# Grid attention: transposing the probabilities in two halves of 64 rows, into two banks, in the tile mode of the scores

## The chip, the core and the metric

The kernel is one program on 1 core of one Trainium2 chip. The metric is the time of an execution on the device in microseconds (us). In the profile, PE is TensorE (PEld its weight loads), DVE is VectorE, ACT is ScalarE, POOL is GpSimd, SP is SyncE.

## The reference

The reference is two transformer blocks, one after the other, on 1024 tokens of width 1024 in float32. The first block has an even layer (window attention with a sink, and differential attention) and an odd layer (latent attention and neighbourhood attention); the second has a dilated attention beside a state-space branch. The change is in the odd layer's neighbourhood attention, called grid in the kernel. Tokens are a grid of 16 rows and 64 columns; eight heads of width 64 attend to 8 x 16 neighbours and to 256 context tokens:

```python
def row_fn(args):
    r, qr = args
    rs = jnp.clip(r - kr_n // 2, 0, rows - kr_n)
    ks = lax.dynamic_slice_in_dim(kg, rs, kr_n, axis=1).reshape(B, n_loc, H, d)
    vs = lax.dynamic_slice_in_dim(vg, rs, kr_n, axis=1).reshape(B, n_loc, H, d)
    ...
    s_loc = jnp.einsum('bqhd,bkhd->bhqk', qr, ks).astype(jnp.float32) * scale + bias[None]
    s_loc = jnp.where(mask, s_loc, NEG)
    s_ctx = jnp.einsum('bqhd,bchd->bhqc', qr, kc).astype(jnp.float32) * scale
    p = jax.nn.softmax(jnp.concatenate([s_loc, s_ctx], axis=-1), axis=-1).astype(v.dtype)
    return (jnp.einsum('bhqk,bkhd->bqhd', p[..., :n_loc], vs)
            + jnp.einsum('bhqc,bchd->bqhd', p[..., n_loc:], vc))
```

## The kernel before

The grid stage works through 32 pairs: four pairs of heads (`hp`), and for each eight blocks of 128 queries (`t`), 8 grid columns of all 16 rows. A pair has two lanes, one head each. Its keys are the neighbouring blocks of 128 and two blocks of context: three and two in the middle (t = 1 to 6), two and two at the edges (t = 0 and 7). One block of keys of one lane is a tile of probabilities, 128 queries x 128 keys, so a pair has ten tiles, or eight at an edge: 24 x 10 + 8 x 8 = 304 tiles.

For each pair:

- `scores` (L1863, PE): for each lane and piece of keys (384 or 256 local ones, then 256 of the context) a product of 64 contracted rows. Lane 0 stands in array rows 0 to 63 and lane 1 in 64 to 127. Each piece has a bank of PSUM, four banks a pair. A product in float32 is two records in the trace (two passes); a transpose is one.
- `minima` (L2963, DVE): adds the bias or mask, scales, writes the row into SBUF (`pair_slot`, in RP) and keeps a running minimum; four a pair, local pieces first, the lanes in turn. It frees the bank.
- `exponential` (L3444, ACT): one for each lane, in place, with the sum in an accumulator column.
- `turn_chunk` (L1876, PE): transposes the tiles, four to a chunk and a bank. The tile is the loaded operand, the identity the one that is streamed.
- `turned_chunks` (L3456 on ACT, L2977 on DVE): copies a chunk from PSUM to one of four slots of 512 columns in RP (`pair_turned`).
- `pair_values` (L1891, PE): products of the values (64 loaded columns) with a turned tile, lane 0 into output partitions 0 to 63 of bank 7, lane 1 into 64 to 127, accumulated over the blocks of keys.
- `pair_outputs` (L3467, ACT): copies the result, 128 x 128, into the block of outputs.

The order of each engine is written by hand. In the step of pair u, PE issues the scores of pair u+1, the values of pair u-1 and the transposes of pair u. DVE does the minima of u+1 and then its copies of u. ACT does the first exponential of u+1, the outputs of u-1, its copies of u and the second exponential of u+1. An engine's queue is strictly in order.

PSUM banks are given out by rings (class `Ring`): `main` has the banks 0 to 4, `turn` the banks 5 and 6. A fill is numbered when the plan is made and waits until the fill that had its bank before was read. `plan_pairs` numbers the fills of `main` in the order: scores of u+1, then what `turns` of u take of it. A pair of ten tiles has three chunks: four tiles in `turn` (read by ACT), four in `turn` (read by DVE), two in `main` (read by ACT). A pair of eight has the first two alone:

```python
cuts = list(range(len(tiles) % 4 if kind == "diff" else 0, len(tiles), 4))
...
if kind in HALVES and c >= 2:
    ch["ring"] = main
elif kind in HALVES:
    ch["f"] = turn.new("dve" if c else "act")
```

A copy also waits until the values have used the chunk that had its slot four chunks before (`s_chunk`). POOL builds the bias tables for a pair of heads (L1270 to L1281) two pairs of heads ahead and stores each finished block of outputs (L1324).

Of the kernel before, what the change touches and what calls it, by code (L numbers as in the profile page):

```python
# [15 lines left out]
ACT = mybir.ActivationFunctionType  # L16
# [3 lines left out]
P = 128  # L20
# [8 lines left out]
HD = 64  # L29
# [85 lines left out]
def build(nc, io, out):  # L115
    x, ctx_in = io["x"][0], io["ctx"][0]
    ctx = ExitStack()
    with ctx:
# [28 lines left out]
        RP = sb("RP", 7168)  # L147
        RX = sb("RX", 3 * 1024)
        RS = sb("RS", 4 * 512)
        ident = sb("ident", P)  # L150
# [21 lines left out]
        ACROSS = ('grid',)  # L172
# [384 lines left out]
        def plan_pairs(kind, pairs, scale, asides=()):  # L557

            todo = list(asides)
            for at, u in enumerate(pairs):  # L560
                u["at"], u["g"] = at, pair_count[0]
                pair_count[0] += 1
                if u["first"]:
                    block_count[0] += 1
                u["block"] = block_count[0] - 1
                u["w"] = sum(pc["w"] for pc in u["pieces"])
                u["aside"], u["turns"] = None, []
                if kind not in ACROSS:
                    divided[0] += 1
                    u["divided"] = divided[0]  # L570
                u["rq"] = new_rms() if kind == "diff" and at == len(pairs) - 1 else None
                tiles = [(lane, P * j, kt) for j, kt in enumerate(u["key_tiles"]) for lane in range(2)]
                if kind == "latent":
                    tiles.sort()
                if kind == "diff":
                    tiles = [x for x in tiles if x[0] == 0]
                cuts = list(range(len(tiles) % 4 if kind == "diff" else 0, len(tiles), 4))
                cuts = ([0] if cuts[0] else []) + cuts + [len(tiles)] if cuts else [0, len(tiles)]
                n = len(cuts) - 1
                for c in range(n):  # L580
                    ch = {"ring": turn, "c": chunk_count[0], "tiles": tiles[cuts[c]:cuts[c + 1]]}
                    if kind in HALVES and c >= 2:
                        ch["ring"] = main
                    elif kind in HALVES:
                        ch["f"] = turn.new("dve" if c else "act")
                    else:
                        ch["f"] = turn.new("act" if c % 2 or (n == 3 and c == 2) or kind == "diff" else "dve")
                    u["turns"].append(ch)
                    chunk_count[0] += 1
                u["turned"] = [[ch for ch in u["turns"] if any(x[0] == lane for x in ch["tiles"])][-1:] for lane in range(2)]  # L590
# [34 lines left out]
            for at, u in enumerate(pairs):  # L625
                if at + 1 < len(pairs):
                    nxt = pairs[at + 1]
                    number_scores(nxt)
                    ask(nxt, at, 4 if kind in HALVES else 6)
                if kind in HALVES:  # L630
                    for c, ch in enumerate(u["turns"][2:]):
                        ch["f"] = main.new("dve" if c else "act")
                    if at >= 2 and kind not in ACROSS:
                        pairs[at - 2]["back"] = main.new("dve")
# [416 lines left out]
        def pair_turned(c):  # L1051

            return RP[:, 5120 + c % 4 * 512:5632 + c % 4 * 512]

        def pair_out(g):

# [392 lines left out]
        def _(pe):  # L1449
# [201 lines left out]
            for si, st in enumerate(stages):  # L1651
# [197 lines left out]
                elif k in PAIRS:  # L1849
# [18 lines left out]
                    def turn_chunk(u, ch):  # L1868
                        if k == "diff":
                            pe.wait_ge(s_mix, u["at"] + 1)  # L1870
                        else:
                            pe.wait_ge(s_pexp, 2 * u["g"] + 1 + max(x[0] for x in ch["tiles"]))
                        ring = ch["ring"]
                        ring.wait_free(pe, ch["f"])
                        for i, (lane, at, _) in enumerate(ch["tiles"]):
                            last = pe.transpose(ring.bank(ch["f"])[:, i * P:(i + 1) * P],  # L1876
# [3 lines left out]
                    def pair_values(u, chunks):  # L1880
# [1 line left out]
                        pe.wait_ge(s_ot, u["g"])  # L1882
                        n_last = len(u["key_tiles"]) - 1
                        for ch in u["turns"][chunks]:
                            ch["ring"].wait_drained(pe, ch["f"])
                            for i, (lane, at, kt) in enumerate(ch["tiles"]):
                                p_t = pair_turned(ch["c"])[:, i * P:(i + 1) * P]
                                vc = u["vc"][lane]
                                first, final = at == 0, at == n_last * P
                                if k in HALVES:  # L1890
# [2 lines left out]
                                else:  # L1893
                                    last = pe.matmul(bank_o[:, P * lane:P * lane + P], p_t, u["v"][:, kt, vc:vc + P],  # L1894
                                                     start=first, stop=final)
                            last.then_inc(s_chunk, 1)

                    def turn_back(u):
                        pe.wait_ge(s_ot, u["g"] + 1)
# [354 lines left out]
        def _(dve):  # L2254
# [429 lines left out]
            for si, st in enumerate(stages):  # L2684
# [241 lines left out]
                elif k in PAIRS:  # L2926
# [40 lines left out]
                    def turned_chunks(u, chunks):  # L2967

                        for ch in chunks:
                            ring = ch["ring"]  # L2970
                            if ring.side[ch["f"]] != "dve":
                                continue
                            ring.wait_full(dve, ch["f"])
# [25 lines left out]
                    def pair_y(u):  # L2999
# [11 lines left out]
                            dve.wait_ge(s_ystore[u["block"] % 2], 16 * (u["block"] // 2))  # L3011
                        dve.wait_ge(s_rec, u["divided"])
                        if k == "latent":
                            dve.wait_ge(s_chunk, u["turns"][-1]["c"] + 1)
                            o = pair_block(st, u["block"])[:, u["y"]:u["y"] + 2 * P].rearrange("p (l c) -> p l c", l=2)
                            r = recips[:, u["at"] % 3, :].unsqueeze(2).broadcast_to([P, 2, P])
                            sig(tt(o, bank_o[:, 0:2 * P].rearrange("p (l c) -> p l c", l=2), r, ALU.mult), s_ot, att_latent["pairs"][0]["g"])
# [122 lines left out]
        def _(act):  # L3140
# [132 lines left out]
            for si, st in enumerate(stages):  # L3273
# [153 lines left out]
                elif k in PAIRS:  # L3427
# [18 lines left out]
                    def turned_chunks(u, chunks):  # L3446

                        for ch in chunks:
                            ring = ch["ring"]
                            if ring.side[ch["f"]] != "act":  # L3450
                                continue
                            ring.wait_full(act, ch["f"])
# [5 lines left out]
                    def pair_outputs(u):  # L3458

                        if k == "latent":  # L3460
                            return
                        act.wait_ge(s_chunk, u["turns"][-1]["c"] + 1)
                        if k == "diff" or k in ACROSS:
                            if u["first"] and u["block"] >= 2:
                                act.wait_ge(s_ystore[u["block"] % 2], 16 * (u["block"] // 2))
# [135 lines left out]
```

## Time and profile before

| | us |
|---|---|
| median of 3 runs | 2604.52 (2602.23 to 2605.28) |
| the profiled execution's own time | 2602.48 |
| its span, first to last instruction | 2600.5 |
| mean granted clock of TensorE, share of full speed | 0.996 |
| PE, DVE, ACT, POOL busy | 2543.1, 1515.0, 799.3, 242.3 |
| grid stage, 1499.40 to 1616.60 of the span | 117.20 |

A matmul's end in the trace is modelled, so starts are what is safe to count: in the timeline the distance from the start of one group of records to the start of the next is what the first one costs PE. Groups of PE are given as engine, line, operands, tile mode (array rows * columns), moved shape and count. The chain of waits goes back from the last instruction to what released it; a bracket `[0.17 <-issue]` is idle time before a group that nothing shown in the profile ended.

### The profile page before, as it was taken

The page shows a single profiled execution, that of the slowest core. Times are in us where ns is not written, and L with a number is a line of the kernel's source. Part 1 is how long each engine was busy: PE and PEld are TensorE (multiplying, and loading weights), DVE is VectorE, ACT ScalarE, POOL GpSimd, SP SyncE. Part 2 cuts the span into 40 slices and gives each one's busy share as a digit, 9 for nine tenths or more (in the row PEclk, how much of TensorE's full clock was granted, in tenths as well). Part 3 has the DMA queues.
Part 4 walks back from the last instruction along what each step waited for, and adds up shares of the span by engine and source line. Part 5 has one row for each costly group of instructions (what it writes and reads, how often), then busy time and mean ns, then how long its engine had stood idle before and what let it go on. Part 6 is the DMA issues. An engine that isn't in the chain of part 4 may idle for free.

```text
span 2600.5 us, 37230 instructions
## 1 busy us (share of the span) xinstructions
PE 2543.1 (98%) x13959; PEld 1865.6 (72%) x13959; DVE 1515.0 (58%) x3827; ACT 799.3 (31%) x1753; POOL 242.3 (9%) x426
## 2 busy tenths in 40 slices
PE   6999999999999999999999999999999999999999
PEld 3477688777778686566688777868578776545867
DVE  2357677599866664344453466757868574515554
ACT  2236511177721123322210066113312364121211
POOL 0100100000001000000042022320000002012000
PEclk9999999999999999999999999999999999999999
DMA  7031000021013121311001010623240104216321
GB/s 262 26 107 46 26 33 33 33 74 56 31 53 110 61 89 57 102 41 41 9 25 39 33 48 34 104 104 114 84 144 33 69 18 122 100 67 241 107 107 54
DMA packets 73857, 190.89 MB, mean 73 GB/s; under 512 B 7260, under 2 KB 10016, under 8 KB 72752
## 3 DMA queue, kind: packets, MB, share of 16 engines
q0 software_dynamic: 27456, 96.97, 11.6%
q1 hardware_dynamic: 45472, 91.16, 10.1%
q8 instruction: 113, 1.85, 0.3%
q14 instruction: 64, 0.52, 0.1%
q10 hardware_dynamic: 752, 0.38, 0.0%
HBM read 145.79 MB, written 43.04 MB: 73 GB/s over the span
## 4 chain that ended last, share of the span: by engine, by line
PE 92%; DVE 3%; issue 2%; ACT 1%; DMA 1%; ACTq 0%; POOL 0%; DVEq 0%; POOLq 0%
PE psum L1501 36%; PE psum L1863 12%; PE psum L1803 8%; PE psum L1876 7%; PE psum L1894 5%; PE psum L1891 5%; PE psum L1979 4%; PE psum L1615 3%; PE psum L1724 2%; PE psum L1487 1%; PE psum L1468 1%; PE psum L2051 1%; PE psum L2069 1%; PE psum L2038 1%; PE psum L1776 1%
## 5 line engine op out<-in xcount | busy, mean ns | idle before, releaser
L3444 ACT ACTIVATE RP<-RP,small 128x1280 f32<-128x1280 f32 (+11 forms) x274 | 252.7, 923 | 195.4 <-DVE small L2963 195.3
L1863 PE MATMUL psum<-RQ 64*128 64x256 f32 (+5 forms) x1344 | 294.5, 495 | 2.3 <-DVE small L2963 1.5
L2963 DVE CUSTOM_DVE_ANT_0 RP<-psum,small 128x512 f32<-128x512 f32 (+1 forms) x382 | 201.6, 573 | 108.8 <-PE psum L1876 86.6
L1803 PE MATMUL psum<-RW,hT 128*128 128x512 f32 (+3 forms) x640 | 231.0, 516 | 1.0 <-ACT hT L3174 1.0
L1863 PEld LDWEIGHTS psum<-RQ 64*128 64x128 f32 (+1 forms) x1344 | 143.4, 187 | 90.0 <-issue 57.8
L1876 PE MATMUL psum<-ident,RP 128*128 128x128 f32 x1388 | 191.6, 279 | 8.8 <-DVE RP L2977 3.6
L3456 ACT ACTIVATE RP<-psum 128x512 f32<-128x512 f32 (+1 forms) x304 | 154.2, 525 | 135.0 <-PE psum L1876 124.7
L1876 PEld LDWEIGHTS psum<-ident,RP 128*128 128x128 f32 x1388 | 150.7, 141 | 60.6 <-issue 52.2
L1803 PEld LDWEIGHTS psum<-RW,hT 128*128 128x128 f32 x640 | 134.5, 215 | 82.3 <-issue 64.6
L1501 PE MATMUL psum<-RW,hT 128*128 128x256 f32 x800 | 181.5, 379 | 0.0
L1501 PEld LDWEIGHTS psum<-RW,hT 128*128 128x128 f32 x800 | 151.7, 190 | 23.3 <-issue 2.2
L1894 PE MATMUL psum<-RQ,RP 128*128 128x128 f32 x1312 | 159.8, 276 | 0.5 <-ACT YR L3470 0.5
L1894 PEld LDWEIGHTS psum<-RQ,RP 128*128 128x128 f32 x1312 | 152.1, 192 | 5.3 <-issue 4.6
L1501 PE MATMUL psum<-RW,RP 128*128 128x256 f32 x640 | 151.3, 379 | 0.0
L2977 DVE COPY RP<-psum 128x512 f32<-128x512 f32 (+1 forms) x144 | 97.1, 675 | 87.8 <-PE psum L1876 87.6
L1501 PEld LDWEIGHTS psum<-RW,RP 128*128 128x128 f32 x640 | 119.3, 190 | 15.0
L1891 PEld LDWEIGHTS psum<-RP,RQ 128*64 128x64 f32 x1856 | 100.1, 137 | 41.2 <-issue 39.1
L1891 PE MATMUL psum<-RP,RQ 128*64 128x128 f32 x1856 | 125.5, 280 | 2.2 <-ACT RP L3456 1.6
L1979 PE MATMUL psum<-RW,hT 128*128 128x512 f32 x256 | 111.7, 594 | 0.0
L1501 PE MATMUL psum<-RW,RQ 128*128 128x256 f32 x480 | 108.8, 379 | 0.0
L1501 PEld LDWEIGHTS psum<-RW,RQ 128*128 128x128 f32 x480 | 90.4, 190 | 12.7 <-issue 1.0
L1501 PE MATMUL psum<-RQ,RP 128*128 128x256 f32 x416 | 93.7, 379 | 0.0
(508 smaller groups left out, 3972.0 us busy)
## 6 DMA issues: line engine op xcount, KB each, us to landing
RW<-in_w_in SPq DMA_DIRECT2D x7, 2048.0 KB, 7.9
RW<-in_od_w_ada SPq DMA_DIRECT2D x6, 2048.0 KB, 7.9
RW<-in_ev_w_in SPq DMA_DIRECT2D x5, 2048.0 KB, 7.9
RW<-in_od_w_in SPq DMA_DIRECT2D x5, 2048.0 KB, 8.0
RQ<-in_ev_w_ada SPq DMA_DIRECT2D x4, 2048.0 KB, 19.4
RX<-in_x POOLq DMA_DIRECT2D x12, 512.0 KB, 7.6
y_even<-YR POOLq DMA_DIRECT2D x20, 256.0 KB, 2.3
RP<-y_even POOLq DMA_DIRECT2D x20, 256.0 KB, 3.5
```

The source lines that it names most:

```text
L1501: last = pe.matmul(main.bank(f)[:, 0:256], lhs(i), rhs[:, i, :], start=i == 0, stop=i == 3)
L1615: last = pe.matmul(main.bank(f), lhs_of("h", j["t"], kk), w_buf(n)[:, kk, :], start=kk == 0, stop=kk == KC - 1)
L1803: last = pe.matmul(main.bank(f)[:, c0:c0 + nc_], lhs_of(st["lhs"], j["t"], kk), w, start=kk == 0, stop=kk == kn - 1)
L1863: last = pe.matmul(main.bank(f)[:, 0:pc["w"]], q, kk[:, keys], start=i == 0, stop=i == len(u["qk"]) - 1)
L1876: last = pe.transpose(ring.bank(ch["f"])[:, i * P:(i + 1) * P], pair_slot(st, u, lane)[:, at:at + P], ident[:, :])
L1891: last = pe.matmul(bank_o[64 * lane:64 * lane + 64, 0:P], u["v"][:, kt, vc:vc + 64], p_t, start=first, stop=final)
L1894: last = pe.matmul(bank_o[:, P * lane:P * lane + P], p_t, u["v"][:, kt, vc:vc + P], start=first, stop=final)
L1979: last = pe.matmul(main.bank(e["m"]), lhs_of("h", e["t"], kk), w_buf(e["w"])[:, kk, :], start=kk == 0, stop=kk == KC - 1)
L2963: drained(main, dve.tensor_tensor_reduce(pair_slot(st, u, lane)[:, pc["at"]:pc["at"] + pc["w"]], main.bank(f)[:, 0:pc["w"]], add, -scale, ...
L2977: drained(ring, dve.tensor_copy(pair_turned(ch["c"])[:, 0:n], ring.bank(ch["f"])[:, 0:n]), ch["f"])
L3444: fn(pr, pr, ACT.Exp, bias=mins[:, at, lane, n - 1:n], scale=-1.0, accum_out=total).then_inc(s_pexp, 1)
L3456: ring.consumed(fn(pair_turned(ch["c"])[:, 0:n], ring.bank(ch["f"])[:, 0:n], ACT.Copy), ch["f"])
```

## The change

In the grid stage alone, a tile's transpose becomes two: the queries 0 to 63 from array rows 0 to 63, and the queries 64 to 127 from rows 64 to 127, each streaming a 64 x 64 identity. These have the shape 64*128 of the scores' tiles. The first halves of a chunk's tiles go into one bank, the second halves into another, 64 columns a tile, so that a bank holds eight half tiles. A pair of eight tiles is one chunk, in the two banks of `turn`. A pair of ten is two chunks: two tiles in two fills of `main`, then eight in the two banks of `turn`. ACT copies the first halves and DVE the second, into the same slots of RP as before, so that the halves stand side by side and `pair_values` reads whole tiles; a chunk counts as two in `s_chunk` and in the slots. The other kinds of attention are left as they are.

```diff
+                if kind in ACROSS:
+                    assert chunk_count[0] % 2 == 0
+                    cuts = [0, len(tiles)] if len(tiles) <= 8 else [0, len(tiles) - 8, len(tiles)]
                 n = len(cuts) - 1
                 for c in range(n):
-                    ch = {"ring": turn, "c": chunk_count[0], "tiles": tiles[cuts[c]:cuts[c + 1]]}
+                    ch = {"ring": turn, "c": chunk_count[0], "tiles": tiles[cuts[c]:cuts[c + 1]], "end": chunk_count[0] + 1}
+                    if kind in ACROSS:
+                        ch["ring"], ch["end"] = main if c < n - 1 else turn, chunk_count[0] + 2
+                        if c == n - 1:
+                            ch["halves"] = [turn.new("act"), turn.new("dve")]
+                            ch["f"] = ch["halves"][1]
+                        u["turns"].append(ch)
+                        chunk_count[0] += 2
+                        continue
...
-                if kind in HALVES:
+                if kind in ACROSS:
+                    for ch in u["turns"][:-1]:
+                        ch["halves"] = [main.new("act"), main.new("dve")]
+                        ch["f"] = ch["halves"][1]
+                elif kind in HALVES:
...
+        def turned_half(ch, half):
+
+            at = 5120 + ch["c"] % 4 * 512
+            v = RP[:, at:at + P * len(ch["tiles"])].rearrange("p (i q) -> p i q", q=P)
+            return v[:, :, HD * half:HD * half + HD]
...
+                        if k in ACROSS:
+                            for f in ch["halves"]:
+                                ring.wait_free(pe, f)
+                            for i, (lane, at, _) in enumerate(ch["tiles"]):
+                                for half, f in enumerate(ch["halves"]):
+                                    rows = slice(HD * half, HD * half + HD)
+                                    last = pe.transpose(ring.bank(f)[:, HD * i:HD * i + HD], pair_slot(st, u, lane)[rows, at:at + P],
+                                                        ident[rows, rows])
+                                    if i == len(ch["tiles"]) - 1:
+                                        ring.written(last)
+                            return
...
                         for ch in u["turns"][chunks]:
-                            ch["ring"].wait_drained(pe, ch["f"])
+                            for f in ch.get("halves", [ch["f"]]):
+                                ch["ring"].wait_drained(pe, f)
                             for i, (lane, at, kt) in enumerate(ch["tiles"]):
-                                p_t = pair_turned(ch["c"])[:, i * P:(i + 1) * P]
+                                p_t = pair_turned(ch["c"] + i // 4)[:, i % 4 * P:(i % 4 + 1) * P]
...
-                            last.then_inc(s_chunk, 1)
+                            last.then_inc(s_chunk, 2 if k in ACROSS else 1)
...
+                            if k in ACROSS:
+                                f = ch["halves"][1]
+                                ring.wait_full(dve, f)
+                                if ch["c"] >= 4:
+                                    dve.wait_ge(s_chunk, ch["c"] - 2)
+                                src = ring.bank(f)[:, 0:HD * len(ch["tiles"])].rearrange("p (i q) -> p i q", q=HD)
+                                drained(ring, dve.tensor_copy(turned_half(ch, 1), src), f)
+                                continue
...
+                            if k in ACROSS:
+                                f = ch["halves"][0]
+                                ring.wait_full(act, f)
+                                if ch["c"] >= 4:
+                                    act.wait_ge(s_chunk, ch["c"] - 2)
+                                src = ring.bank(f)[:, 0:HD * len(ch["tiles"])].rearrange("p (i q) -> p i q", q=HD)
+                                ring.consumed(fn(turned_half(ch, 0), src, ACT.Copy), f)
+                                continue
...
-                        act.wait_ge(s_chunk, u["turns"][-1]["c"] + 1)
+                        act.wait_ge(s_chunk, u["turns"][-1]["end"])
```

The order on PE in the middle of the grid stage, pairs of ten tiles, before. A row is line, operation, operands and the shape of the output, and how often; a product counts once here, though it is two records in the trace. L1863 are the scores of the next pair, L1891 the values of the pair before, L1876 the transposes:

```order
L1876 MATMUL psum<-ident,RP 128x128 x10
L1863 MATMUL psum<-RQ 128x384 x2
L1863 MATMUL psum<-RQ 128x256 x2
L1891 MATMUL psum<-RP,RQ 64x128 x10
L1876 MATMUL psum<-ident,RP 128x128 x10
```

And with the change, where the scores have the line L1884, the values L1924 and the transposes L1901:

```order
L1901 MATMUL psum<-ident,RP 128x64 x20
L1884 MATMUL psum<-RQ 128x384 x2
L1884 MATMUL psum<-RQ 128x256 x2
L1924 MATMUL psum<-RP,RQ 64x128 x10
L1901 MATMUL psum<-ident,RP 128x64 x20
```

The sequence of scores, values and transposes stays; ten transposes of 128 columns become twenty of 64.

The order on ACT at the same place, before (L3444 are the exponentials, L3467 the outputs, L3456 the copies):

```order
L3444 ACTIVATE RP,gate<-RP,small 128x640 x2
L3467 ACTIVATE RQ<-psum 128x128
L3456 ACTIVATE RP<-psum 128x512
L3456 ACTIVATE RP<-psum 128x256
L3444 ACTIVATE RP,gate<-RP,small 128x640 x2
```

and with the change (L3485 exponentials, L3516 outputs, L3497 copies):

```order
L3485 ACTIVATE RP,gate<-RP,small 128x640 x2
L3516 ACTIVATE RQ<-psum 128x128
L3497 ACTIVATE RP<-psum 128x2x64
L3497 ACTIVATE RP<-psum 128x8x64
L3485 ACTIVATE RP,gate<-RP,small 128x640 x2
```

The two exponentials that a row counts together are the second of one pair and the first of the next. The copy of the large chunk moves behind that of the small one. DVE has, behind its four minima, a copy of 128x2x64 and one of 128x8x64, where it had one of 128x512.

## Rows read from the trace of the kernel before

**Rows 1.** The page: engines (busy us, share, instructions) and the chain that ended last.

```profile
PE 2543.1 (98%) x13959; PEld 1865.6 (72%) x13959; DVE 1515.0 (58%) x3827; ACT 799.3 (31%) x1753; POOL 242.3 (9%) x426
...
PE 92%; DVE 3%; issue 2%; ACT 1%; DMA 1%; ACTq 0%; POOL 0%; DVEq 0%; POOLq 0%
```

**Rows 2.** Stretches: start:end, length; PE, PEld, DVE, ACT, POOL busy; PEclk; DMA share, GB/s.

```profile
1499.40:1616.60 117.20, 115.88 (x1169) 87.80 (x1168) 80.23 (x290) 81.93 (x215) 25.81 (x43) 1.00 0.11 36
...
1540.27:1544.03 3.76, 3.76 (x39) 2.83 (x38) 2.54 (x10) 2.65 (x8) 3.41 (x9) 1.00 0.03 7
...
1560.74:1561.77 1.03, 1.03 (x11) 0.86 (x9) 0.61 (x4) 0.79 (x2) 0.00 (x0) 1.00 0.00 0
1551.56:1552.62 1.06, 1.06 (x9) 0.69 (x8) 0.80 (x2) 1.06 (x3) 0.00 (x0) 1.00 0.24 47
```

**Rows 3.** The chain in order of time: start, length, engine, line, count.

```profile
1540.34 1.28 PE psum L1863 x8
1541.62 1.24 PE psum L1891 x20
1542.86 1.24 PE psum L1876 x10
```

**Rows 4.** Waits in the grid stage: us in total, times, longest.

```profile
PEld psum L1891 <- issue: 10.8, 32, 0.5
PEld psum L1863 <- issue: 5.3, 31, 0.3
PEld psum L1876 <- issue: 5.3, 31, 0.2
```

**Rows 5.** Timeline of PE after the stage: transposes between products of one mode.

```profile
1638.40 0.60 PE L1487 MATMUL psum<-ident,RS 128*128 128x128 f32 x4
1638.84 1.89 PE L1501 MATMUL psum<-RW,RP 128*128 128x256 f32 x8
```

**Rows 6.** Groups of the grid stage, by shape: busy us, mean ns, idle before.

```profile
L1876 PE MATMUL psum<-ident,RP 128*128 128x128 f32 x304 | 40.2, 279 | 0.9 <-ACT RP L3444 0.9
L1891 PEld LDWEIGHTS psum<-RP,RQ 128*64 128x64 f32 x608 | 32.5, 136 | 10.9 <-issue 10.8
L1863 PEld LDWEIGHTS psum<-RQ 64*128 64x128 f32 x256 | 22.6, 186 | 12.1 <-issue 5.3 <-DVE small L2963 0.4
L2977 DVE COPY RP<-psum 128x512 f32<-128x512 f32 x32 | 22.1, 691 | 24.8 <-PE psum L1876 24.8
L3467 ACT ACTIVATE RQ<-psum 128x128 f32<-128x128 f32 x31 | 8.0, 257 | 0.4 <-PE psum L1891 0.4
```

**Rows 7.** Short products in two other stages: timeline of PE, and groups.

```profile
1905.79 0.57 PE L1550 MATMUL psum<-RQ,ident 128*16 128x16 f32 x16
...
2262.48 2.06 PE L2022 MATMUL psum<-RQ 64*128 64x128 f32 x32
...
L1550 PE MATMUL psum<-RQ,ident 128*16 128x16 f32 x16 | 0.6, 177 | 0.0
...
L2022 PE MATMUL psum<-RQ 64*128 64x128 f32 x32 | 2.1, 278 | 0.0
```

**Rows 8.** Timeline of ACT and DVE over one pair of ten tiles.

```profile
1542.81 0.83 ACT L3444 ACTIVATE RP<-RP,small 128x640 f32<-128x640 f32 x1 [1.11 <-DVE small L2963]
1543.64 0.26 ACT L3467 ACTIVATE RQ<-psum 128x128 f32<-128x128 f32 x1
1543.80 0.58 ACT L3456 ACTIVATE RP<-psum 128x512 f32<-128x512 f32 x1
...
1541.33 0.56 DVE L2963 CUSTOM_DVE_ANT_0 RP<-psum,RX 128x384 f32<-128x384 f32 x1 [0.47 <-PE psum L1863]
1543.92 0.69 DVE L2977 COPY RP<-psum 128x512 f32<-128x512 f32 x1 [0.74 <-PE psum L1876]
```

**Rows 9.** Timeline of POOL: building the tables of the last pair of heads.

```profile
1563.03 2.13 POOL L1270 TENSOR_SCALAR RS<-RS 128x768 f32<-128x768 f32 x1
...
1570.59 0.10 POOL L1281 MEMSET small<- 128x1 f32 x1
```

More of the change, by code:

```diff
@@ L3013, in pair_y @@
                         if k == "latent":
-                            dve.wait_ge(s_chunk, u["turns"][-1]["c"] + 1)
+                            dve.wait_ge(s_chunk, u["turns"][-1]["end"])
                             o = pair_block(st, u["block"])[:, u["y"]:u["y"] + 2 * P].rearrange("p (l c) -> p l c", l=2)
```

## Prediction

> Words used below: S is a pair's score products, V its value products, T its transposes (turns), M the four running minima on DVE, E0 and E1 the two exponentials on ACT, H a fill of the five-bank ring that holds transposes. S+1.06 means 1.06 us after a pair's S began.
>
> **What bounds the kernel now.** The page's first part comes first: PE is busy for 98% of the span, DVE for 58%, ACT for 31%, and the chain that ended last is 92% PE [rows 1]. So time is saved where PE's own stream gets shorter, and only there. The change touches one stage, so the view by stretches comes next: the grid attention runs from 1499.40 to 1616.60, 117.2 us, PE busy for 115.9 of them, at a granted clock of 1.00 (the 2.4 GHz level) [rows 2]. The chain inside it consists of PE alone, in three kinds of piece in turn: S 1.28, V 1.24, T 1.24, together 3.76 us for a pair with ten tiles [rows 3]. Its large waits are on no other engine: the list has "issue" 31 or 32 times ahead of the weight loads of each of the three lines [rows 4]. DVE works 2.54 and ACT 2.65 of the 3.76 [rows 2], so a shorter T is worth its length until the pair comes down to what their chains allow.
>
> **The parts of a piece.** T with ten tiles takes 1.24, with eight 1.03 [rows 2, 3]: 0.107 a tile (rounded from 0.105, and a little more in the starts), and 0.17 that belongs to no tile. V is alike: twenty records in 1.24. S with 384-column pieces takes 1.28, with 256 alone 1.06 [rows 2, 3]. A lane streams two passes of each piece, so 256 more columns cost 0.22, or 0.00085 a column; T's 0.107 over 128 columns is 0.00084. The price goes with the streamed columns. S's 4 x 256 columns a lane make 0.86 of 1.06: again about 0.20 that is nobody's. In grid attention each piece has another tile mode than its neighbour: 64*128 for S, 128*64 for V, 128*128 for T. Where transposes stand beside products of their own mode, four take from 1638.40 to 1638.84, 0.44, which is 4 x 0.11, and nothing is left over [rows 5]. So the 0.17 to 0.20 is the price of a change of mode together with the first weight load, which nothing hides.
>
> **The change, term by term.**
>
> (a) *The boundary from T to S.* T's halves have S's mode, so this change of mode goes: three in a round become two. Of S's 0.20 the drain goes wholly. The first weight load now runs beside the last half's 0.054 of streaming; a 128-column load takes 186 ns and a 64-column one 136 [rows 6], so 128 columns are about 0.10 of loading and 0.05 of it stays. Saved 0.15. T is followed by S 30 times (32 pairs, but no S is left behind the last two): **4.5 us**. T still pays its 0.17 behind V.
>
> (b) *The halves.* Each of 304 tiles [rows 6] becomes two records that stream 64 columns of the identity, 64 x 0.00084 = 0.054, one in rows 0 to 63, one in rows 64 to 127, into different banks. No row of before shows a transpose in a 64-row tile, so the price is bounded. The nearest row is L2022: 64*128 products with 128-column loads, 32 in 2.06, one lasting 0.28; first to last start is 1.78 over 31 steps, 0.057 each, though each streams 128 columns (0.107) [rows 7]. Two row halves therefore run at once, loads hidden. The good end is the issue of records: L1550 streams only 16 columns, 16 records in 0.57, (0.57 - 0.18)/15 = 0.026 each [rows 7], 0.052 for a tile's two. The bad end is no overlap and no hidden load: 0.054 of streaming and 0.054 of loading each, 0.215 a tile. I take the value of L2022's kind, both halves at once, 0.054 a tile. That saves 0.0535 on each of 304 tiles: **16.3 us**. At 0.052 it is 16.7.
>
> (c) *Evacuation.* The third chunk of a ten-tile pair (256 columns, ACT) goes, and the 512-column chunks of ACT and DVE stay as 8 x 64; each engine gets one copy of 2 x 64 = 128 columns. ACT copies 128 columns from PSUM in 257 ns now (L3467) [rows 6], so ACT has about 0.1 less work. DVE gains a copy: 691 ns for 512 columns [rows 6] bounds it from above; for 128 I estimate 0.3. DVE's 2.54 becomes 2.8 of a pair of some 3.1. It fits, and costs nothing as long as DVE's order does: M, both copies, next M. The copies follow T's last landing, about S+0.3, and end near S+1.1; M starts at S+1.06 (1540.27 to 1541.33) [rows 8]. The cover is just used up.
>
> (d) *The ring.* A ten-tile pair takes six fills of the five main banks instead of five. S's fourth piece then waits for ACT's copy of H's first half, and V and the next T are queued behind it on PE. ACT's order: E0 starts at S+2.54 (1542.81) and lasts 0.83, the output of the pair before takes 0.16 until the next start, the copy 0.26 [rows 8]: done at S+3.79, and with the semaphore and a late M at S+3.85. The next S begins at S+3.08 (3.76 less 0.15 and 0.53) and comes to its fourth piece 0.75 later, S+3.83. This is a tie. I charge 0.06 to 0.08 on each of the 24 ten-tile pairs, **1.9 us**; the ends are 0 and the rival below. H's second half needs M's first minimum, at S+1.6, before T at S+2.5: no wait. V finds ACT's copies done near S+1.05, before its S+1.28; T finds E1 done near S+1.75.
>
> (e) *POOL* builds the third and fourth bias tables in 7.7 us from 1563.03 [rows 9], eight pairs ahead of their use; eight pairs still last over 23 us. The stages behind the grid start from its end and shift as they are.
>
> Sum: 4.5 + 16.3 - 1.9 = 18.9 us. The profiled execution took 2602.5 (span 2600.5), so 2583.6; the median of the three runs is 2604.5, 2.0 above it: **2585.6**.
>
> **The rivals.**
>
> *The copies become the bound.* If M starts 0.3 later behind the copies, E0, the copy of H and the fourth piece follow, and so does the next M: a ten-tile pair settles near 3.4 instead of 3.08. Then 24 x 0.36 and, for pairs with eight tiles, which have no H, 8 x (0.15 + 8 x 0.0535) = 4.6 are left, 13.2 in all: 2591. For it: the ties in (c) and (d). Against it: ACT waits 1.11 and DVE 0.74 and 0.47 in a pair [rows 8]. The Trainium skill (TensorEngine Tiling, PSUM Bottleneck) says that tiling speeds up TensorE but not the emptying of PSUM, which may then become the bottleneck; no run here shows it yet, and by it the time is this rival's. Chance 0.12.
>
> *Half of the gain per tile.* The loads are partly exposed and a tile costs 0.08: 304 x 0.027 = 8.2, with (a) 12.7: 2592. Or the halves overlap but a transpose beside a product still drains: (a) goes, 2590. The trace speaks against the second, though in the 128-row mode [rows 5]. Chance 0.11 together.
>
> *Records are issued one by one.* V has twenty records in 1.24, as T would have; if twenty loads with twenty products can't come faster than V's, 0.055 a record, a tile still costs 0.107 and (a) alone is left: 2600. L1550's 0.026 speaks against it. The Trainium skill (TensorE: Matmul & The Clock Gate, "Wait — 56ns, not 53.3ns?") gives a floor of about 25 ns from start to start, and about 62 ns a matmul where firmware decodes; by the 62 ns a tile would cost 0.124 and the time would be some 2605, and L1550's 0.026 does not agree with that. Chance 0.10.
>
> *Slower.* The transposes of the two halves neither overlap nor hide their loads: one after the other, 2 x 0.107 = 0.215 a tile, 304 x 0.108 = +32.8, less 4.5: 2633. It decides from 0.122 a tile on, where (a) is used up. For it: no row shows a transpose in this mode. Against it: L2022 does both with a longer load. Chance 0.05.
>
> **How the numbers follow.** The forecast case, 2580 to 2589, has 0.62. What a measurement can tell from no change here is 0.2%, 5.2 us. Faster by more: forecast, copies, half gain: 0.62 + 0.12 + 0.11 = 0.85. Within: issue, 0.10. Slower: 0.05. The range runs from full cover without the tie of (d) and at 0.052 a tile (2604.5 - 4.5 - 16.7 = 2583.3, or 2581.8 if nothing of S's first load stays, and the runs lie up to 2.3 us beside their median) up past 2592, with the same scatter: 2580 to 2596. It leaves out 0.15 and the forecast case's tails.
>
> **What would show it.** Right: 608 transposes of 64*128 with 64 columns, their starts in twos a few ns apart; T of ten tiles at about 0.7 and no "issue" gap between T and S; a ten-tile pair at 3.1; the stage at 98 us. (d) shows as a gap inside S, ended by ACT's copy. Wrong: T at 1.07 and more (issue or no overlap), or T at 0.7 and a wait of PE on DVE or ACT of over 0.3 in each pair (copies).

## The result, and the profile after

The changed kernel takes 2588.58 us, median of four runs (2585.25 to 2591.41), beside 2604.88 for the kernel before on the same chip. The ratio is 0.9943, 95% interval 0.9929 to 0.9957: faster by 0.4 to 0.7%, or 16.3 us by the medians. Forecast were 2585.6 (18.9 us less) and a range of 2580 to 2596. The profiled execution took 2585.25, with a span of 2583.2 at a mean granted clock of 0.997.

The page after the change, engines and the chain that ended last, beside [rows 1]:

```profile
PE 2524.3 (98%) x14263; PEld 1854.8 (72%) x14263; DVE 1521.1 (59%) x3851; ACT 795.9 (31%) x1753; POOL 242.3 (9%) x426
...
PE 93%; DVE 3%; ACT 1%; issue 1%; DMA 0%; ACTq 0%; DVEq 0%
```

PE has 304 more instructions and is busy 18.8 us less; it bounds the kernel as before. The stretches, beside [rows 2] (start:end, length; PE, PEld, DVE, ACT, POOL busy; PEclk; DMA share, GB/s): the grid stage, and one pair of ten tiles in it.

```profile
1497.35:1599.09 101.74, 99.23 (x1473) 76.97 (x1472) 86.39 (x314) 79.14 (x215) 25.82 (x43) 1.00 0.13 42
1538.14:1541.28 3.14, 3.14 (x50) 2.47 (x49) 2.78 (x11) 2.51 (x7) 2.79 (x6) 1.00 0.24 52
```

The stage lasts 101.74 instead of 117.20, at the same granted clock of 1.00 (the 2.4 GHz level). That is 15.46 of the 17.23 us between the two profiled executions. Another 2.06 lie ahead of the stage, where the code is the same, and are scatter: in the profiled executions of all kernels with that code the stage begins between 1497.35 and 1503.35. Behind it 0.2 are lost. So the stage is where to look. Its lines are now L1884 for the scores (S), L1901 for the halves (T), L1924 for the values (V), L3497 and L3010 for the copies on ACT and DVE, L2996 for the minima. The timeline of PE's weight loads over two pairs of ten tiles (start, length, engine, line, operation, tile mode, shape, count, idle time before): the distance between two starts is what a piece costs PE.

```profile
1538.14 0.70 PEld L1901 LDWEIGHTS psum<-ident,RP 64*128 64x128 f32 x20 [0.17 <-issue]
1538.75 0.95 PEld L1884 LDWEIGHTS psum<-RQ 64*128 64x128 f32 x8
1540.04 1.07 PEld L1924 LDWEIGHTS psum<-RP,RQ 128*64 128x64 f32 x20 [0.33 <-issue]
1541.28 0.70 PEld L1901 LDWEIGHTS psum<-ident,RP 64*128 64x128 f32 x20 [0.17 <-issue]
1541.90 1.00 PEld L1884 LDWEIGHTS psum<-RQ 64*128 64x128 f32 x8
1543.23 1.07 PEld L1924 LDWEIGHTS psum<-RP,RQ 128*64 128x64 f32 x20 [0.33 <-issue]
```

The timeline of PE shows which scores these are, pieces of 384 columns in the first pair and of 256 alone, those of an edge pair, in the second:

```profile
1538.81 1.29 PE L1884 MATMUL psum<-RQ 64*128 64x384 f32 x8
...
1541.96 1.35 PE L1884 MATMUL psum<-RQ 64*128 64x256 f32 x8
```

T is 0.61 (1538.14 to 1538.75) where it was 1.24 [rows 3], V is 1.24 as before. The S with 384 columns is 1.29 where it was 1.28; the one with 256 is 1.33 where it was 1.06 [rows 2], so a stall of 0.27 lies in it. The bracket ahead of the scores is gone: their loads start while the last halves still stream. Ahead of V 0.33 and ahead of T 0.17 are left, the other two changes of mode. The list of waits in the stage says the same, beside [rows 4], and holds one line that before had not:

```profile
PEld psum L1924 <- issue: 10.9, 30, 1.0
PEld psum L1901 <- issue: 5.3, 31, 0.2
PE psum L1924 <- DVE RP L3010: 1.4, 2, 0.9
...
PEld psum L1884 <- issue: 0.3, 1, 0.3
```

"Issue" ahead of the scores falls from 5.3 us in 31 waits to 0.3 in one. The new line is at the stage's end (timeline of PE):

```profile
1594.53 0.44 PE L1924 MATMUL psum<-RP,RQ 128*64 128x128 f32 x4
1595.43 1.09 PE L1924 MATMUL psum<-RP,RQ 128*64 128x128 f32 x16 [0.46 <-DVE RP L3010]
1596.46 0.71 PE L1901 MATMUL psum<-ident,RP 64*128 64x64 f32 x16
1598.07 1.09 PE L1924 MATMUL psum<-RP,RQ 128*64 128x128 f32 x16 [0.90 <-DVE RP L3010]
```

No scores stand between the last transposes and the last values, so PE sits through the copies there. The groups by shape, beside [rows 6], give the prices:

```profile
L1901 PE MATMUL psum<-ident,RP 64*128 64x64 f32 x608 | 25.8, 228 | 0.9 <-ACT RP L3485 0.9
...
L3010 DVE COPY RP<-psum 128x512 f32<-128x512 f32 x32 | 22.1, 691 | 9.5 <-PE psum L1901 9.3
...
L3010 DVE COPY RP<-psum 128x128 f32<-128x128 f32 x24 | 7.0, 291 | 2.9 <-PE psum L1901 2.0
...
L3497 ACT ACTIVATE RP<-psum 128x128 f32<-128x128 f32 x24 | 6.4, 266 | 0.0
```

**Where the stage's 15.46 us come from.** Start to start, summed over the stage: T 38.56 before and 20.00 after, S 40.56 and 42.87, V 38.08 and 38.87. T's two sizes split it by tile and by piece: ten tiles cost 1.243 before and 0.616 after, eight cost 1.025 and 0.490. Per tile that is (1.243 - 1.025)/2 = 0.109 before and 0.063 after, so 0.046 is saved on each; of the piece's own 0.153 before nothing is left (0.490 - 8 x 0.063 = -0.014), so 0.167 is saved on each of the 30 pieces that scores follow. Those 30 hold 286 tiles: 30 x 0.167 + 286 x 0.046 = 18.2. The last two pairs, T and V together, go from 5.15 to 5.41. S loses 2.3, the other V 0.1. These are lengths between the starts of loads. S's first load now starts 0.06 ahead of its product, so between the starts of products T falls by 16.8 and S loses only 0.7; their sum is nearly the same either way.

| | forecast | measured |
|---|---|---|
| (a) boundary T to S | -4.5 (0.15 each) | -5.0 (0.167 each) |
| (b) halves | -16.3 (304 x 0.0535) | -13.2 (286 x 0.046) |
| last two pairs | part of (b) | +0.3 |
| (c) copies | 0 | 0, but for the last pairs |
| (d) ring, seen in S | +1.9 | +2.3, of which 1.65 is the ring (below) |
| V of the other pairs | 0 | +0.1 |
| stage | -18.9 | -15.5 |

### The profile page after: what moved, and what is told of

It is laid out like the page before. It is cut to its first block, busy times and chain, and to the rows that moved or that the text cites. A ratio compares the mean times of both kernels' runs of the same rounds, so it can differ in the third digit from the quotient of the medians.

```text
span 2583.2 us, 37879 instructions
## 1 busy us (share of the span) xinstructions
PE 2524.3 (98%) x14263; PEld 1854.8 (72%) x14263; DVE 1521.1 (59%) x3851; ACT 795.9 (31%) x1753; POOL 242.3 (9%) x426
## 4 chain that ended last, share of the span: by engine, by line
PE 93%; DVE 3%; ACT 1%; issue 1%; DMA 0%; ACTq 0%; DVEq 0%
PE psum L1522 36%; PE psum L1884 11%; PE psum L1824 8%; PE psum L1908 6%; PE psum L1927 5%; PE psum L1924 5%; PE psum L2012 4%; PE psum L1745 3%; PE psum L1636 3%; PE psum L1508 1%; PE psum L1489 1%; PE psum L2084 1%; PE psum L2102 1%; PE psum L2071 1%; PE psum L1901 1%
## 5 line engine op out<-in xcount | busy, mean ns | idle before, releaser
L3485 ACT ACTIVATE RP<-RP,small 128x1280 f32<-128x1280 f32 (+11 forms) x274 | 252.7, 923 | 180.8 <-DVE small L2996 180.7
L1884 PE MATMUL psum<-RQ 64*128 64x256 f32 (+5 forms) x1344 | 293.8, 493 | 2.3 <-DVE small L2996 1.5
L2996 DVE CUSTOM_DVE_ANT_0 RP<-psum,small 128x512 f32<-128x512 f32 (+1 forms) x382 | 201.6, 573 | 108.8 <-PE psum L1908 86.5
L1884 PEld LDWEIGHTS psum<-RQ 64*128 64x128 f32 (+1 forms) x1344 | 145.9, 187 | 83.8 <-issue 52.6
L3505 ACT ACTIVATE RP<-psum 128x512 f32<-128x512 f32 (+1 forms) x248 | 128.2, 530 | 134.1 <-PE psum L1908 124.1
L1908 PE MATMUL psum<-ident,RP 128*128 128x128 f32 x1084 | 151.3, 279 | 7.9 <-DVE RP L3018 3.6
L1908 PEld LDWEIGHTS psum<-ident,RP 128*128 128x128 f32 x1084 | 118.1, 141 | 54.0 <-issue 46.9
L1924 PEld LDWEIGHTS psum<-RP,RQ 128*64 128x64 f32 x1856 | 100.0, 137 | 42.3 <-issue 39.0
L1924 PE MATMUL psum<-RP,RQ 128*64 128x128 f32 x1856 | 125.3, 279 | 3.6 <-DVE RP L3010 1.4
L3018 DVE COPY RP<-psum 128x512 f32<-128x512 f32 (+1 forms) x112 | 74.9, 670 | 63.0 <-PE psum L1908 62.7
```

Of the source, the lines that this page charges most:

```text
L1884: last = pe.matmul(main.bank(f)[:, 0:pc["w"]], q, kk[:, keys], start=i == 0, stop=i == len(u["qk"]) - 1)
L1924: last = pe.matmul(bank_o[64 * lane:64 * lane + 64, 0:P], u["v"][:, kt, vc:vc + 64], p_t, start=first, stop=final)
L2996: drained(main, dve.tensor_tensor_reduce(pair_slot(st, u, lane)[:, pc["at"]:pc["at"] + pc["w"]], main.bank(f)[:, 0:pc["w"]], add, -scale, ...
L3485: fn(pr, pr, ACT.Exp, bias=mins[:, at, lane, n - 1:n], scale=-1.0, accum_out=total).then_inc(s_pexp, 1)
L3505: ring.consumed(fn(pair_turned(ch["c"])[:, 0:n], ring.bank(ch["f"])[:, 0:n], ACT.Copy), ch["f"])
```

## The experiments

The theory at this point: two row halves run at once and save 0.046 a tile, not 0.0535; standing in S's mode saves one drain in each pair; a sixth fill of the five banks costs what S loses; the last copies cost about a microsecond. The rivals give the gain to the chunks and copies instead of the halves, put the price of a change of mode at next to nothing, and see no dependence on the order of the halves. Edits are shown against the changed kernel. The first four ran together, beside 2604.6 for the kernel before, and the last three beside 2604.47. Stage lengths come from the profiled executions and tell smaller steps apart than the medians do: pieces without a stall repeat within 0.01 us from pair to pair and from run to run.

### All first halves, then all second halves

```diff
-for i, (lane, at, _) in enumerate(ch["tiles"]):
-    for half, f in enumerate(ch["halves"]):
+for half, f in enumerate(ch["halves"]):
+    for i, (lane, at, _) in enumerate(ch["tiles"]):
```

> The change with one thing turned round: of each chunk all first halves are transposed, then all second halves, so that neighbours stand in the same 64 array rows. Banks, copies, waits and the number of records stay. Theory (the halves gain because two of them, in different array rows, run at once; the profile of the change has their starts in twos, 0.062 us from two to two): twenty records now follow one another at 0.054 to 0.062, the transposes of a ten-tile pair take 1.1 to 1.25 instead of 0.62, the stage grows from 101.7 us by 14 to 19, the time is 2602 to 2608. Rival (the gain comes from the shorter stream, the bigger chunks or the copies, whatever the rows): the transposes stay at 0.62 to 0.7 and the time within 3 us of 2588.6.

Measured: 2597.5 (ratio to before 0.9976, 0.9961 to 0.9991), the stage 109.14, 7.4 longer. Neither number was met: the order matters, but half as much as the theory said. T sums to 29.06 instead of 20.00, while S gives back 1.6, since the ring's stalls vanish in the longer pair. The timeline of PE over one pair of ten tiles shows why it is only half:

```profile
1537.73 0.95 PE L1901 MATMUL psum<-ident,RP 64*128 64x64 f32 x17
1538.46 0.59 PE L1884 MATMUL psum<-RQ 64*128 64x384 f32 x1
1538.52 0.35 PE L1901 MATMUL psum<-ident,RP 64*128 64x64 f32 x3
1538.71 1.29 PE L1884 MATMUL psum<-RQ 64*128 64x384 f32 x7
1539.93 1.31 PE L1924 MATMUL psum<-RP,RQ 128*64 128x128 f32 x20
```

T and S take 2.20 (1537.73 to 1539.93), 0.30 more than in the pairs without a stall of the changed kernel (1538.14 to 1540.04, above). The first score product, of lane 0 in rows 0 to 63, starts at 1538.46, ahead of three transposes in rows 64 to 127 that stand before it in PE's program. The second halves do the same to the first ones: in the single records the first run of eight has starts 0.062 apart, and the second run sets in 7 ns behind its fifth record (1538.153 and 1538.160). From the first record of this chunk to the scores in rows 64 to 127 (1537.904 to 1538.707) it takes 13 steps of 0.062 instead of 8; the five more are 0.31, which is the whole loss. So the overlap is shown to be what saves, and the two halves reach past each other by three records (the sixth to eighth here). A strict order would have cost about 20 x 0.062 = 1.24, an estimate from this pitch.

### Whole transposes in the new chunks

```diff
-for half, f in enumerate(ch["halves"]):
-    rows = slice(HD * half, HD * half + HD)
-    last = pe.transpose(ring.bank(f)[:, HD * i:HD * i + HD], pair_slot(st, u, lane)[rows, at:at + P],
-                        ident[rows, rows])
+m = len(ch["tiles"]) // 2
+f = ch["halves"][i // m]
+last = pe.transpose(ring.bank(f)[:, P * (i % m):P * (i % m) + P],
+                    pair_slot(st, u, lane)[:, at:at + P], ident[:, :])
...
```

(Each engine copies half of the tiles instead of half of each tile.)

> The chunks, banks, fills, copies and waits of the change, but each tile is transposed whole, in the 128*128 mode: half of a chunk's tiles into one bank, half into the other. Theory (all of the gain is PE's: the change of mode between transposes and scores, 4.5 us, and the overlap of halves, some 14): nothing of the gain is left; the transposes take 1.24 again, and the stage is 117 to 121 us, since the waits in the scores and at the end of the stage may stay; time 2604 to 2609. Rival (fewer and larger chunks, or the new split of the copies, are part of the gain): 2590 to 2600.

Measured: 2607.15 (ratio 1.0007, 0.9996 to 1.0017), the stage 118.25, against 117.20 before. Chunks, banks, numbers of fills and sizes of copies are the changed kernel's, and nothing is gained: the theory's numbers, and not the rival's. The loads show the drain again, and S without stall (1.28):

```profile
1540.18 1.07 PEld L1901 LDWEIGHTS psum<-ident,RP 128*128 128x128 f32 x10 [0.17 <-issue]
1541.42 0.95 PEld L1884 LDWEIGHTS psum<-RQ 64*128 64x128 f32 x8 [0.17 <-issue]
1542.70 0.42 PEld L1924 LDWEIGHTS psum<-RP,RQ 128*64 128x64 f32 x8 [0.33 <-issue]
```

The last values cost more here too: V of the last pair but one 1.97 (1.28 before), T of the last 1.94 (1.41). The stage's 1.05 over before is theirs, and since no halves are left here, the new chunks cause it.

### A whole transpose among the halves

```diff
+if len(ch["tiles"]) == 2 and i == 1:
+    pe.transpose(ring.bank(ch["halves"][0])[:, 256:384], pair_slot(st, u, lane)[:, at:at + P], ident[:, :])
```

One more transpose in each ten-tile pair, which nobody reads, in the mode 128*128, between the first tile's halves and the rest.

> The change with one more record in each of the 24 ten-tile pairs: between the two tiles of the small chunk a whole tile is transposed once more, in the 128*128 mode, into unused columns of the bank; nobody reads it. The record streams 128 columns, 0.107 us, and PE changes its mode twice more. Theory (a change of mode costs 0.17 to 0.20, drain and first load): 0.4 to 0.5 for each of the 24, 10 to 12 us in all, 2598 to 2601. Rival (the gap of before between transposes and scores was a wait for data, and a change of mode costs next to nothing): 0.11 to 0.15 for each, 3 to 4 us, 2591 to 2593.

Measured: 2596.17 (ratio 0.9965, 0.9954 to 0.9975), the stage 109.79, 8.05 longer than the changed kernel's. The time is some 2 us under the theory's range and above the rival's. The timeline of PE:

```profile
1543.65 0.28 PE L1903 MATMUL psum<-ident,RP 64*128 64x64 f32 x2
1543.86 0.33 PE L1900 MATMUL psum<-ident,RP 128*128 128x128 f32 x1
1544.12 0.77 PE L1903 MATMUL psum<-ident,RP 64*128 64x64 f32 x18
1544.73 1.30 PE L1884 MATMUL psum<-RQ 64*128 64x384 f32 x8
```

T of ten tiles goes from 0.616 to 1.02. Of these 0.40 the added record's own price is 0.109, so the two changes of mode cost 0.29, 0.147 each. Each of the 24 pairs pays the theory's 0.40, 9.7 in all; 1.6 come back in S, whose stalls go in the longer pair, and the theory left that out. The 0.147 is (a)'s price measured by itself: forecast 0.15, and 0.167 by the split above. The Trainium skill (TensorEngine Tiling, Key Properties) says that a change of mode drains TensorE, one of tile alone does not; the runs agree, with 0.147 for the first and no gap for the second.

### The two banks of the ring in the other order

```diff
-ch["halves"] = [main.new("act"), main.new("dve")]
-ch["f"] = ch["halves"][1]
+ch["f"] = main.new("dve")
+ch["halves"] = [main.new("act"), ch["f"]]
```

(PE issues the halves in the order of their banks.)

> The change with the two fills of the five-bank ring in the other order: the second half's fill, copied by DVE, is numbered and finished first. The next pair's fourth score piece then needs DVE's early copy and not ACT's, which stands behind an exponential and an output. Theory (the scores that take 1.34 to 1.45 instead of 1.28 wait for ACT's copy): all scores of 384 columns take about 1.28, the stage loses 1 to 2 us, the time is 2586.5 to 2588. Rival (they wait for DVE's late minima, or PE itself): scores as before, the time within 0.7 us of 2588.6.

Measured: 2587.11 (ratio 0.9935, 0.9918 to 0.9951), the stage 100.08, 1.66 less than the changed kernel's. S sums to 41.22 instead of 42.87. Loads of two pairs in the stretch where the changed kernel's S stalls:

```profile
1544.23 0.95 PEld L1884 LDWEIGHTS psum<-RQ 64*128 64x128 f32 x8
1545.52 1.07 PEld L1924 LDWEIGHTS psum<-RP,RQ 128*64 128x64 f32 x20 [0.33 <-issue]
1546.76 0.70 PEld L1901 LDWEIGHTS psum<-ident,RP 64*128 64x128 f32 x20 [0.17 <-issue]
1547.38 0.74 PEld L1884 LDWEIGHTS psum<-RQ 64*128 64x128 f32 x8
```

The S with 384 columns (1544.23) keeps its 1.29, and the one with 256 (1547.38) is 1.07 instead of 1.33. Over the stage every S behind a pair of ten tiles is back at 1.28 or 1.07, as the theory said. The fourth score piece now takes the bank that DVE read, and DVE's small copy comes ahead of its large one. So 1.65 of the 2.3 us of S were (d), the wait for ACT's copy of H. The records of the changed kernel say the same: 23 S follow the halves of a ten-tile pair; in 12 of them ACT's small copy ends 0.59 to 0.68 after the first score product, and these stall; in the other 11 it ends at most 0.55 after it, and none stalls. In the shown S with 256 columns the copy ends at 1542.555 and the fourth piece starts at 1542.607.

The cost is uneven: eight of the 12 lose 0.05 to 0.13, and the four with 256 columns, which come to their fourth piece 0.2 earlier, lose 0.26 each, 1.05 of the 1.65. Of the 0.66 that stays, 0.47 is in the four S behind the edges (0.06 to 0.18 each). In three of these the next V starts 0.10 after ACT's copy of eight half tiles, where the other V of the 30 pairs start 0.19 or more after ACT's last copy; so V seems to wait for that copy there, which no run tested.

### Equal chunks in the last two pairs, alone and with the ring's order

```diff
+if at >= len(pairs) - 2:
+    cuts = [0, len(tiles) // 2, len(tiles)]
```

> In the last two pairs of the stage the tiles are cut into two chunks of equal halves instead of one of 2 and one of 8, so that the last copies have 4 or 5 tiles to move instead of 8. The theory: at the end of the stage no scores stand between transposes and values, and the values wait for VectorE's copy of the large chunk (waits of 1.4, 0.5 and 0.9 us behind L3010 in the changed kernel's trace); with a 4-tile copy of about 0.43 us in place of the 0.69 us one the two last values shrink by 0.3 to 0.5 us each, and the stage by 0.5 to 1.0 us to 100.7 to 101.2. The rival, that these waits come from the exponentials and not from the copies, expects the stage at 101.7 as before. Outside the stage nothing changes.

> The order of the two banks of the five-bank ring swapped (VectorE's half first), and the last two pairs cut into equal chunks, both together. If the two costs are separate, the gains add: 1.5 to 1.7 us from the ring and 0.5 to 1.0 us from the end, a stage of 99.1 to 99.6 us and 2586 to 2587 us. If the ring's stall only moves to another wait once the end is changed, the stage stays at 100.1 us or more.

Measured alone, one execution of 2586.94: the stage 100.95, 0.79 less, as the theory said; a single time says nothing about so small a step. With the ring's order 2586.46 (ratio 0.9934, 0.9920 to 0.9947), the stage 99.17: 2.57 less than the changed kernel's, and 0.91 less than with the ring's order alone. Separate costs would give 1.66 + 0.79 = 2.45, so they add up. The end of the stage with both (timeline of PE):

```profile
1597.01 1.31 PE L1926 MATMUL psum<-RP,RQ 128*64 128x128 f32 x20 [0.36 <-ACT RP L3499]
1598.25 0.71 PE L1903 MATMUL psum<-ident,RP 64*128 64x64 f32 x16
1599.32 1.09 PE L1926 MATMUL psum<-RP,RQ 128*64 128x128 f32 x16 [0.36 <-DVE RP L3012]
```

V of the last pair but one falls from 1.95 to 1.27 and T of the last from 1.59 to 1.04, while T of the last but one, which now ends in a wait, grows from 0.82 to 1.17. Together the four go from 5.41 to 4.53; a wait of 0.36 for the copies remains in each pair.

### The same in the window and dilated stages

The plan, the halves and the copies as above for all three stages, VectorE's half first in the ring as in the fourth run; in the two others the transpose of the outputs moves ahead of the halves, so that halves and scores are neighbours:

```diff
+BY_HALVES = ('window', 'grid', 'dilated')
...
+if i >= 2 and k not in ACROSS and k in BY_HALVES:
+    turn_back(ps[i - 2])
 for ch in u["turns"]:
     turn_chunk(u, ch)
-if i >= 2 and k not in ACROSS:
+if i >= 2 and k not in ACROSS and k not in BY_HALVES:
     turn_back(ps[i - 2])
...
```

(Not shown: the ring numbers the fill of that transpose ahead of the halves' fills, and VectorE's division of the outputs moves ahead of its copies.)

> The same halves in the two other stages of this form (window and dilated attention), with the back transpose of the outputs moved ahead of the halves so that halves and scores stand side by side, and VectorE's half first in the five-bank ring in all three stages. If a ten-tile row of transposes falls from 1.24 to 0.62 us there as it did here, 336 tiles of the window stage and 288 of the dilated one give 0.0625 us each, 39 us in all; 0 to 10 us come back in ring stalls, since five banks now take seven fills a pair, and in the first and last pairs. That makes 2549 to 2560 us. The rival, that the two stages are bound by VectorE once TensorE is shorter (it also divides the outputs there), expects less than half of it, 2568 to 2587 us.

Measured: 2562.77 (ratio 0.9841, 0.9828 to 0.9855), 41.7 us under the kernel before and 24.3 under the run with the ring's order alone, whose grid stage it shares. It is past the end of the theory's 2560 and under the rival's 2568: neither range was met, and the gain was forecast too large. The stretch of the window stage, from the first to the last load of its scores, in the changed kernel:

```profile
165.42:306.00 140.58, 139.51 (x1338) 103.44 (x1340) 103.78 (x396) 92.44 (x253) 13.56 (x48) 1.00 0.17 60
```

and with this edit:

```profile
169.36:295.33 125.97, 123.36 (x1666) 87.82 (x1667) 110.09 (x426) 89.32 (x252) 13.56 (x48) 1.00 0.19 68
```

It is 14.6 shorter. PE is busy for 123.36 of 125.97 and DVE for 110.09, so PE still bounds the stage, and the rival has fallen. T's sum falls by 14.3, from 35.88 to 21.60 for 336 tiles: 0.0425 a tile. I had expected 0.0625, the grid's gain of a whole piece divided by its tiles, and a boundary's 0.167 is in that. Here no boundary goes. The output's transpose stood behind T in the same mode before, and now stands ahead of the halves in a mode of its own:

```profile
239.63 0.14 PEld L1937 LDWEIGHTS psum<-ident,RS 128*128 128x128 f32 x1 [0.17 <-issue]
239.89 0.70 PEld L1904 LDWEIGHTS psum<-ident,RP 64*128 64x128 f32 x20
240.51 0.95 PEld L1887 LDWEIGHTS psum<-RQ 64*128 64x128 f32 x8
241.79 1.07 PEld L1927 LDWEIGHTS psum<-RP,RQ 128*64 128x64 f32 x20 [0.33 <-issue]
```

One transpose costs 0.26 there (239.63 to 239.89), its 0.109 and a change of mode. The dilated stage is 9.4 shorter, at a mean granted clock of 0.93 against 0.97 in the changed kernel, so the clock may hide a part of its gain; the two were not separated. This kernel is the fastest of those run. The ring gives little back: S in the window stage sums to 48.7 against 47.4, with seven fills of five banks in a pair.

## Why the prediction was right, and where its sizes were off

**What bounds it.** Right: PE alone bounds the stage before and after, and the gain is T's length.

**(a) Boundary.** Right in mechanism, 0.15 forecast, 0.167 by T's lengths and 0.147 for a change of mode by itself. It was expected to shorten S. Between the starts of loads it is seen in T, since S's first loads now start ahead of T's end; between the starts of products 0.05 of it is in S.

**(b) Halves.** The two halves do run at once: in the changed kernel the single records start in twos about 1 ns apart. The mis-sized term is "0.054 a tile", taken from the price per streamed column: a tile costs 0.062 from one pair of starts to the next (1538.254, .316, .378, .440). With a price before of 0.109, where 0.107 was taken, the saving is 0.046 and not 0.0535: 2.1 us less on 286 tiles. The 18 tiles of the last two pairs, which the step counted in full, are 1.0 more; together that is the step from 16.3 to 13.2. Each load starts some 6 ns after the product before it, and the next product comes some 55 ns after that load, so the loads may be a part of it. The first experiment shows the same 0.062 in one half of the rows alone, so the halves do not slow each other down. Whether the loads set the pitch or something else that is common to all of these records was not tried. A part could be read from L2022, on which the step rested [rows 7]: 0.057 a record is 0.115 for two, which stream 0.107 side by side, and in the single records the pairs follow one another 0.112 apart (2262.807, 2262.919, 2263.031). So two row halves cost 5 to 8 ns more than their streaming there too, and the step put that at nothing.

**(c) Copies.** DVE's small copy takes 291 ns, estimated at 0.3, and V waits for no copy in the ordinary pairs (the three behind the edges apart), though DVE is busy for 2.78 of 3.14. The rival, in which M starts 0.3 later and a ten-tile pair takes 3.4, has fallen: in the pair shown M starts at S+1.07 (1538.75 to 1539.82), and the pair takes 3.14. Missing in the step was the stage's end: behind the last two T there are no scores to cover the copies. Some 1.1 us were lost (18 tiles x 0.046 = 0.83 expected, 0.26 longer measured), and equal chunks bring 0.8 to 0.9 of that back. By the Trainium skill (TensorEngine Tiling, PSUM Bottleneck) the emptying of PSUM may become the bottleneck; the runs agree with it for these last pairs, with 1.4 us of waits, and for the ring in (d), but not for the stage as a whole.

**(d) Ring.** Right in mechanism, the tie between ACT's copy and the fourth piece: 1.9 forecast, and 1.65 gone when the fourth piece takes the other bank. The profile names no releaser for these waits; the swap of the banks and the ends of the copies do. That the sum came so near is in part luck: 0.06 to 0.08 was charged on each of 24 pairs, but 12 stall, and most of it lies in four S with 256 columns, which the step did not look at.

**Rivals.** Records issued one by one would have made T 1.07 and more, a half gain 0.08 a tile; measured were 0.062 to 0.063. The Trainium skill (TensorE: Matmul & The Clock Gate, "Wait — 56ns, not 53.3ns?") gives about 62 ns a matmul where firmware decodes; the trace has two transposes in that time, so the figure does not hold here as a limit on issue. The slower case needed 0.122 a tile and was far off.

## What to carry to other kernels

When a transpose or another short product stands between products of a 64-row mode, it can be split into row halves that go to two banks and alternate record by record: here this saved 0.046 us a tile, and 0.15 to 0.17 more for each change of mode that really goes, which must be counted boundary by boundary and not folded into a price per tile. After the change look for the two places where the cover ran out: the ring whose next fill now waits for the slower reader (swap the order of its banks), and the end of the stage, where nothing stands between the copy and its user (make the last chunks equal).

## What the runs showed of the hardware

- PE's products need not start in the order of the program when they stand in different row halves: a score product in rows 0 to 63 started ahead of three transposes in rows 64 to 127 that the program has before it (1538.46 and 1538.52 to 1538.65). That an engine's queue is strictly in order, as said of the kernel before, does not hold for PE in this way. The Trainium skill (TensorE: Matmul & The Clock Gate, The mechanism) says that weight loads are pulled ahead of matmuls, and that matmuls start and end in the program's order; in this trace the starts are not in order, and the ends are modelled.
- Float32 transposes in two row halves, 64 columns each, cost 0.062 a pair and the same 0.062 when one half of the rows works alone; a whole 128 x 128 one costs 0.109.
- A change between the modes 64*128 and 128*128 costs 0.147, the mean of two, measured by a transpose of the second mode put among halves of the first.
